# Differential attention: projection units in the order keys, queries, values instead of keys, values, queries

## The reference, cut to what matters

```python
def project(h, rotary):
    q, k, v = jnp.split(h @ w_qkv, [DIFF_QK_WIDTH, 2 * DIFF_QK_WIDTH], axis=-1)
    q = rmsnorm(q.reshape(bsz, -1, 2, DIFF_HEADS, HEAD_DIM), q_norm)
    k = rmsnorm(k.reshape(bsz, -1, 2, DIFF_HEADS, HEAD_DIM), k_norm)
    if rotary:
        q, k = apply_rope(q, cos, sin), apply_rope(k, cos, sin)
    return q, k, v.reshape(bsz, -1, DIFF_HEADS, DIFF_V_DIM)
...
s = jnp.einsum("bqmhd,bkmhd->bmhqk", q, k) * (HEAD_DIM ** -0.5)
p = jax.nn.softmax(s, axis=-1)
a = (p[:, 0] - lam * p[:, 1]).astype(v.dtype)
return jnp.einsum("bhqk,bkhd->bqhd", a, v)
```

## Time and profile before

| | us |
|---|---|
| median of 3 runs (lowest, highest) | 3165.74 (3163.70, 3170.12) |
| profiled execution, its own time | 3154.95 |
| its span | 3152.8 |
| PE busy | 3034.3 (96%) |
| DVE busy | 1748.1 (55%) |
| POOL busy | 1419.0 (45%) |
| ACT busy | 1093.7 (35%) |
| granted PE clock, mean | 0.983 |

### The profile page before, as it was taken

How to read it: one execution, slowest core, us unless ns; L and a number is a source line. 1 busy time by engine, 2 the same in 40 slices (tenths; PEclk the granted TensorE clock), 3 DMA queues, 4 the chain that set the end, 5 groups by cost and what they waited for, 6 DMA issues and landing times.

```text
span 3152.8 us, 44415 instructions
## 1 busy us (share of the span) xinstructions
PE 3034.3 (96%) x16112; PEld 2575.0 (82%) x16112; DVE 1748.1 (55%) x2983; ACT 1093.7 (35%) x1553; POOL 1419.0 (45%) x1692
## 2 busy tenths in 40 slices
PE   8799999999999999999998989899999999999999
PEld 6697668888888879999998787567988877898887
DVE  6568874555555516878887724664433344343333
ACT  4432324444444433333333433454322122231211
POOL 5143444444444446878842223001545554655553
PEclk9899999999999999999999999999999999999999
DMA  6034774555555558999995212100333322232322
GB/s 190 21 101 140 276 284 166 183 187 187 188 187 188 184 199 301 344 364 343 363 370 212 74 41 74 34 1 1 107 101 95 98 94 80 81 107 94 100 87 80
DMA packets 181436, 498.54 MB, mean 158 GB/s; under 512 B 17432, under 2 KB 68760, under 8 KB 178712
## 3 DMA queue, kind: packets, MB, share of 16 engines
q1 hardware_dynamic: 87728, 311.69, 29.6%
q10 hardware_dynamic: 71016, 117.45, 10.5%
q0 software_dynamic: 22528, 67.19, 5.7%
HBM read 431.78 MB, written 64.49 MB: 157 GB/s over the span
## 4 chain that ended last, share of the span: by engine, by line
PE 87%; DVE 6%; DMA 3%; ACT 2%; POOL 2%; issue 2%; ACTq 0%; SPq 0%; DVEq 0%
PE ps L584 25%; PE ps L585 24%; PE ps L586 24%; PE ps L807 3%; PE ps L981 2%; PE ps L968 2%; PE ps L775 2%; PE ps L994 1%; DVE nb L1980 1%; DMA abuf<-act_dram 1%; DMA unit_raw<-w_units 1%; POOL value_rows L552 1%; POOL picked L544 1%; PE ps L784 1%; DVE std L1591 1%
## 5 line engine op out<-in xcount | busy, mean ns | idle before, releaser
L526 POOL TENSOR_TENSOR unit_lo<-unit_raw,unit_hi 128x256 fp32r<-128x256 f32 x1432 | 1058.5, 773 | 1554.7 <-ACT unit_hi L1108 1554.0
L584 PE MATMUL ps<-hn_hi,unit_hi 128*128 128x512 f32 (+1 forms) x2344 | 922.2, 393 | 33.3 <-DVE hn_lo L1606 15.9
L585 PE MATMUL ps<-hn_lo,unit_hi 128*128 128x512 f32 (+1 forms) x2344 | 898.5, 383 | 0.0
L586 PE MATMUL ps<-hn_hi,unit_lo 128*128 128x512 f32 (+1 forms) x2344 | 898.2, 383 | 0.0
L1108 ACT ACTIVATE unit_hi<-unit_raw 128x1024 fp32r<-128x1024 f32 x486 | 505.9, 1055 | 465.9 <-DMA unit_raw<-w_units 357.9
L584 PEld LDWEIGHTS ps<-hn_hi,unit_hi 128*128 128x128 f32 x2344 | 444.7, 190 | 161.1 <-issue 42.2
L586 PEld LDWEIGHTS ps<-hn_hi,unit_lo 128*128 128x128 f32 x2344 | 444.0, 189 | 86.7
L585 PEld LDWEIGHTS ps<-hn_lo,unit_hi 128*128 128x128 f32 x2344 | 445.0, 190 | 83.1 <-issue 3.8
L584 PE MATMUL ps<-gp_hi,unit_hi 128*128 128x384 f32 x1024 | 344.0, 336 | 7.7 <-DVE gp_lo L1911 7.6
L585 PE MATMUL ps<-gp_lo,unit_hi 128*128 128x384 f32 x1024 | 342.9, 335 | 0.0
L586 PE MATMUL ps<-gp_hi,unit_lo 128*128 128x384 f32 x1024 | 342.8, 335 | 0.0
(11 more groups left out here) (276 smaller groups left out, 4264.7 us busy)
## 6 DMA issues: line engine op xcount, KB each, us to landing
unit_raw<-w_units SPq DMA_DIRECT2D x486, 512.0 KB, 3.6
araw<-ada_units SPq DMA_DIRECT2D x96, 512.0 KB, 5.7
act_dram<-stage ACTq DMA_DIRECT2D x32, 1024.0 KB, 6.3
gate_dram<-gst ACTq DMA_DIRECT2D x16, 1536.0 KB, 6.7
gbuf<-gate_dram ACTq DMA_DIRECT2D x16, 1536.0 KB, 22.0
abuf<-act_dram ACTq DMA_DIRECT2D x32, 768.0 KB, 8.7
x<-x_t SPq DMA_DIRECT2D x8, 256.0 KB, 5.8
picked<-act_dram,act_at POOLq DMA_INDIRECT x128, 7.1
```

The lines of the kernel that those rows point to most:

```text
L526: last = nc.gpsimd.tensor_tensor(lo[:, u % RING, cols], raw[:, u % RING, cols], hi[:, u % RING, cols].bitcast(F32), ALU.subtract)
L584: mm(dst, wh, ah, start=start, stop=False)
L585: mm(dst, wh, al, start=False, stop=False)
L586: return mm(dst, wl, ah, start=False, stop=stop)
```

## The change

The 8 query units are taken before the 8 value units. The weights keep their order in memory; SP loads the two groups from exchanged addresses. `behind(s)` becomes a plain run: squares of tile s-1 up to s = 16, rotation of tile s-2 up to s = 17. So the squares of tile 15 and the rotation of tile 14 stand behind value group 1, the rotation of tile 15 behind value pair 0, and none is left between the projections and the attention. Value group j writes bank (j+2)%4; its waits name copies of query tiles. The scores of step 0 wait for the last value copy and all head tiles, and VectorE's first maximum follows the last rope. The split context rows move to 64 and 72 KB, the place of `stage`, which served the gelu stage of the expert layer.

```diff
 def behind(s):
-    kind, n = s // DC, s % DC
-    if kind == 0:
-        return (n - 1 if n >= 1 else None), (n - 2 if n >= 2 else None)
-    if kind == 1:
-        return (DC - 1 if n == 0 else None), (DC - 2 + n if n < 2 else None)
-    return (DC + n - 1 if n >= 1 else None), (DC + n - 2 if n >= 2 else None)
+    if s > 2 * DC + 1:
+        return None, None
+    return (s - 1 if 1 <= s <= 2 * DC else None), (s - 2 if s >= 2 else None)
...
-        cn_hi = at("cn_hi", R1, [P, DC, TC], F32R)
-        cn_lo = at("cn_lo", R1 + 8 * KB, [P, DC, TC], F32R)
+        cn_hi = at("cn_hi", 64 * KB, [P, DC, TC], F32R)
+        cn_lo = at("cn_lo", 72 * KB, [P, DC, TC], F32R)
...
# SP
-            load_range(U_PEER + RING + P - TAIL_UNITS, N_UNITS)
+            load_range(U_PEER + RING + P - TAIL_UNITS, U_DIFF + DC)
+            for n in range(DC):
+                load_unit(U_DIFF + DC + n, of=U_DIFF + 2 * DC + n)
+            for n in range(DC):
+                load_unit(U_DIFF + 2 * DC + n, of=U_DIFF + DC + n)
+            load_range(U_DIFF + 3 * DC, N_UNITS)
...
# TensorE
+            for n in range(DC):
+                pe.wait_ge(hd_ev, DC + n - 1)
+                project(U_DIFF + DC + n, ps[:, n % 2, :], hn_hi, hn_lo)
+                behind_unit(DC + n)
             for n in range(0, DC, 2):
-                u = U_DIFF + DC + n
+                u = U_DIFF + 2 * DC + n
...
                     if j < 4:
-                        pe.wait_ge(hd_ev, DC)
+                        pe.wait_ge(hd_ev, (DC, DC, 2 * DC - 1, 2 * DC)[j])
...
-                    dst = ps[:, j % 4, 0:2 * P].rearrange("p (h v) -> p h v", h=2)
+                    dst = ps[:, (j + 2) % 4, 0:2 * P].rearrange("p (h v) -> p h v", h=2)
...
-                    if t == 0:
-                        behind_unit(DC + n)
+                    if t == 1:
+                        behind_unit(2 * DC + n)
                 pe.wait_ge(v_done, KTS * (n // 2 + 1))
                 pe.sem_inc(unit_used, 2)
-                behind_unit(DC + n + 1)
-            for n in range(DC):
-                if n < 2:
-                    pe.wait_ge(v_ev, KTS * DC // 2)
-                else:
-                    pe.wait_ge(hd_ev, DC + n - 1)
-                project(U_DIFF + 2 * DC + n, ps[:, n % 2, :], hn_hi, hn_lo)
-                behind_unit(2 * DC + n)
-            head_squares(2 * DC - 1)
-            rotate(2 * DC - 2)
+                behind_unit(2 * DC + n + 1)
...
-            pe.wait_ge(hd_ev, 2 * DC)
-            pe.wait_ge(hd_done, DC + DC // 2 + 1)
-            at_scores(0)
-            rotate(2 * DC - 1)
             pe.wait_ge(hd_done, 2 * DC)
             pe.wait_ge(v_ev, KTS * DC // 2)
+            at_scores(0)
...
# VectorE
             for m in range(2 * DC + 1):
                 if m < 2 * DC:
                     head_norm(m)
-                else:
-                    at_max(0)
                 if m:
                     rope(m - 1)
-
+            at_max(0)
```

More of the change, by code:

```diff
@@ L442, in _, with load_unit @@
         def _(sp):
-            def load_unit(u, per=0, i=None):
+            def load_unit(u, per=0, i=None, of=None):
                 s = u % RING
@@ L448, in load_unit @@
                         sp.wait_ge(unit_used, u - RING + 1)
-                    src = w_units[u]
+                    src = w_units[u if of is None else of]
                 else:
@@ L1460, in _ @@
                 behind_unit(n)
+            for n in range(DC):
+                used(U_DIFF + DC + n)
+                head_evict(DC + n, n)
+                behind_unit(DC + n)
             for n in range(0, DC, 2):
@@ L1464, in _ @@
                     act.wait_ge(v_done, j + 1)
[L1465 to L1474, removed]
+                    activation(Vd[n][:, t, :], ps[:, (j + 2) % 4, 0:P], ACT.Copy)
+                    activation(Vd[n + 1][:, t, :], ps[:, (j + 2) % 4, P:2 * P], ACT.Copy).then_inc(v_ev, 1)
+                    if t == 1:
+                        behind_unit(2 * DC + n)
+                behind_unit(2 * DC + n + 1)
             act.wait_ge(lam_s, 1)
```

## The result

The changed kernel took 3150.39 us (median of 5 runs, 3132.43 to 3155.93), the kernel before beside it 3170.12 (5 runs, 3163.70 to 3172.69); the ratio is 0.9935, 95% interval 0.9906 to 0.9963. The forecast was 3151 and a ratio of 0.9953.

A forecast was written before the change was run, and what follows sets the result against it. The query stage was taken as bound by the ScalarE-VectorE round, not TensorE. Terms 12.10 + 59.00 + 67.54 + 13.35 = 151.99 against 166.73 saved 14.7 us, giving 3151 from the median 3165.74; range 3143 to 3159.

The forecast's parts named there:

- Step 1: Kernel before, from S(7) to the scores of step 3: the old path takes 166.73 us.
- Step 2: From key tile 7's squares to query tile 8's: 12.10 us with low clock at the first, 10.73 at full clock.
- S(7): S(m) is the squares matmul of head tile m, 0 to 7 keys, 8 to 15 queries; the forecast counts from S(7).
- Step 3: Squares of tile 8 to those of tile 15: the same seven rounds as before, 59.00 us, about 0.6 idle left at the end.
- Step 4: Squares of tile 15 to the end of the values: 67.54 us, with the last query rounds covered by value groups.
- the old tail, 12.6: Roots, reciprocals and updates of tiles 14 and 15 beside the value groups: would cost 12.6 us if that cover were gone.
- R(14): R(m) is the turn (rotation) matmul of head tile m; R(14) was to stand behind value group 2.
- Step 5: End of values to scores of step 3: 13.35 us, table load hidden; the skill's drain would make it 1.1 us longer.
- Step 6: Waits, queues and loads in the stage: covered; the context rows at another address cost nothing.
- waited for weights: Hidden rival: saving returns as other waits, a query unit late for weights by 7.5 us or the attention's start; 3160.3, chance 0.08.
- does what it says: Rival: last query tiles' work not inside the values, tail of 12.6 us stays, near 3163.6; counted within the hidden chance, 0.08.
- the rival wanted 0.5: Slower rival: clock stays at half through the query units, net 37 us slower, 3203; chance 0.04.

The follow-up runs named there:

- The second measurement: The changed kernel run again, unaltered, against the kernel before: ratio 0.9954, interval 0.9928 to 0.9980.
- the lighter rounds: Changed kernel without the reciprocal of the eight query tiles: 143.88 us from S(7) to the scores of step 3, against 151.95 in the changed kernel.
- the filled gap: Changed kernel with 18 extra matmuls between query unit 0 and S(7): 151.27 us from S(7) to the scores of step 3.
- the kernel with the last rounds behind the values: Changed kernel with squares of tile 15 and turns of tiles 14 and 15 after the last value group: 160.51 us from S(7) to scores of step 3.
- mixed_a: Changed kernel with three value pairs moved forward among key and query units, squares and turns placed anew: ratios to the kernel before 0.9875 and 0.9889.
- mixed_b: Changed kernel with one value pair alone moved between key unit 7 and query unit 0, squares and turns placed anew: ratio to the kernel before 0.9920.

## Why the prediction was right

It was right in the direction, and in the stage in mechanism and size: 151.99 us forecast, 151.95 and 151.98 measured. That the time came out at 3150.39 for 3151 is luck in part: the two medians lie 19.7 us apart, 5.0 more than forecast, but the kernel before came out 4.4 above the median on which the forecast was set. The second measurement, 0.9954, lies nearer to its 0.9953 than the first. By its steps:

- **Step 1 and what bounds the stage.** That the query rounds are bound by ScalarE and VectorE and TensorE alone needs 7.4 is shown by the lighter rounds, but for its size (52.39 us for seven, 7.2 each at full clock).
- **Step 2**, S(7) to S(8): 12.10 forecast, 12.09 measured, low clock at S(7) included, behind 2.86 us of idle. The other bound, 10.73, came in the filled gap and, with 2.88 us of idle, by itself in the kernel with the last rounds behind the values. So the choice between the bounds was a matter of the single execution, worth 1.36 us, and that it hit was luck. The length of idle, by which it was made, does not decide: the matmul behind 2.55 us that kept full clock in the earlier trace rows took 1.22 instead of 0.70 in the changed kernel, at a clock of 0.50:

```profile
1736.74 1.22 PE L612 MATMUL ps<-std,con 128*128 128x256 f32 x2 [2.55 <-DVE std L1583]
```

  Nor is the early S(8) always worth the whole 1.37: in the filled gap and in the lighter rounds the clock fell behind S(8), and in the filled gap this took half of it back.
- **Step 3**, seven rounds: 59.00 and 59.03; idle before S(15) 0.6 and 0.60.
- **Step 4**, S(15) to the end of the values: 67.54, measured 67.57 (the last value matmul started at 1967.96 and took 0.28). The cover was priced at "the old tail, 12.6" if it were gone, which was too dear: taking it away cost 10.0, and with an end as in the kernel before it would have been about 6.6 by the estimate above. S(15), R(14) and R(15) then leave the values, which the price leaves out.
- **Step 5**, the start: 13.35 and 13.26. The table load was hidden as forecast; the first exponential waited 0.24 us for the maximum, not for the load:

```profile
1969.69 1.28 ACT L1470 ACT_TABLE_LOAD   x1
1970.98 0.20 ACT L1470 ACTIVATE lamt<-lamt 128x2 f32<-128x2 f32 x1
1971.43 0.90 ACT L1480 ACTIVATE Ed<-ps,stats 128x768 f32<-128x768 f32 x1 [0.24 <-DVE stats L1991]
```

  The drain that the Trainium skill (ScalarE: Activation LUTs, What ACT_TABLE_LOAD costs) counts beside each load isn't in these rows either: 0.01 us lie between the load's end and the small exponential.
- **Step 6**, the rows' address at nothing: ratio 0.9987 with 1 in the interval, and the stage at 166.29; for the stage this holds, for the rest within the interval.
- **The rivals.** No square and no scores (L882, L965) waited for weights, and no projection shows a wait for them in this stage either. R(15) stands among the value matmuls (1914.28), so the code does what it says. The clock was 1.00 through the query units, where the rival wanted 0.5. The prediction put that rival under a rule of the Trainium skill (TensorE: Matmul & The Clock Gate, HAM oscillation — how this bites in real kernels) that does not reach it: the kernel told of there waited some 3 to 5 us at each turn, the query units here 0.6 to 1.35, so these rows neither bear that page out nor speak against it.

What the prediction could not give is the 22.6 us between the two spans. It set the sum on the median and its range wide by the scatter of the runs; the expert stage alone moved by 36 us between profiles of these kernels.

## What to carry to other kernels

Where a chain over ScalarE and VectorE binds some units of a stage and other units need TensorE alone, the second kind belongs between the first, not behind it. The idle before the chain's own matmuls, read from the table of waits, tells where there is something to gain; the gain itself was larger than the idle removed, 14.8 us for 9.0 in the changed kernel and 18.0 more for 13.3 in the mixed one, since TensorE's busy time fell too. Count such a stage from one event to another in its own profile: the stage repeated to 0.03 us in the changed kernel and to 0.42 in the mixed one, while S(7) itself moved by 24 us between the two profiles of the changed kernel.

## What the runs showed of the hardware

- Idle of TensorE between 2 and 3 us may be followed by low clock or not, with the same instructions around it: 2.86 and 2.88 before S(7) by low clock in both profiles of the changed kernel, 2.88 there by full clock in the kernel with the last rounds behind the values; 2.55 before the matmul of std by full clock in the kernel before and by low clock in the changed one. Once 1.99 us was enough: in the kernel with the lighter rounds S(6) took 2.04 behind it, where 2.01 left S(6) at 1.10 in the changed kernel.
- Two short gaps together behaved like that too. Idle of 0.63 and 2.04 us with 1.56 us of scores between left the clock up in both profiles of the changed kernel (scores of step 1 in 2.44) and took it down in both of mixed_a (3.81 and 3.58) and in mixed_b (3.32). From the scores of step 1 to those of step 3 it was 11.07 us in mixed_a and 9.03 in the changed kernel.
- Full clock at one gap need not bring the whole gain: with the gap before S(7) filled, the clock fell behind S(8), one round later (R(7) in 1.75 us instead of 1.02), and the stage gained 0.7 us instead of 1.35. That this is the rule is not shown.
